# Delta-rule heads: the norm rows of a head taken two quarters at a time early in the next head, the decay sums in other banks, four K tiles ahead of the first head's sums

## What is computed

```python
def gated_deltanet(q, k, v, z, b, a, conv_w, a_log, dt_bias, norm_w):
    qkv = jax.nn.silu(causal_conv(jnp.concatenate([q, k, v], axis=-1), conv_w))
    qc = l2norm(qc.reshape(shp)) * (DN_HEAD_DIM ** -0.5)
    kc = l2norm(kc.reshape(shp))
    beta = jax.nn.sigmoid(b)
    g = -jnp.exp(a_log) * jax.nn.softplus(a + dt_bias)
    o = chunk_gated_delta_rule(qc, kc, vc, g, beta)
    o = o * lax.rsqrt(jnp.mean(o * o, axis=-1, keepdims=True) + EPS) * norm_w
    o = o * jax.nn.silu(z)
    return o

def chunk_gated_delta_rule(q, k, v, g, beta):   # per chunk
    g = jnp.cumsum(g, axis=-1)
    decay = jnp.exp(jnp.where(tril, g[..., :, None] - g[..., None, :], -jnp.inf))
    L = jnp.where(strict, (k_beta @ k.T) * decay, 0.0)
    T = triangular_solve(eye + L, eye)
    ...                                         # then the scan over the chunks
```

## Time and profile before

| | |
|---|---|
| median of 3 runs | 2531.49 us (2530.45 to 2532.93) |
| the profiled execution, its own time | 2530.18 us |
| its span | 2528.4 us |
| PE busy | 2388.7 us, 94% |
| DVE busy | 1877.6 us, 74% |
| ACT busy | 943.8 us, 37% |
| POOL busy | 1068.0 us, 42% |
| mean granted clock of TensorE | 0.985 |

### The profile page before, as it was taken

One profiled execution on the slowest core, in us unless ns is written; L12 is line 12 of the kernel. 1 busy time (PEld: TensorE's weight loads), 2 busy tenths in 40 slices (PEclk: granted clock), 3 DMA queues, 4 the chain that ended last, 5 costly groups with the idle time before them and its releaser, 6 DMA issues.

```text
span 2528.4 us, 38471 instructions
## 1 busy us (share of the span) xinstructions
PE 2388.7 (94%) x15284; PEld 1902.2 (75%) x15284; DVE 1877.6 (74%) x2356; ACT 943.8 (37%) x1488; POOL 1068.0 (42%) x675
## 2 busy tenths in 40 slices
PE   8887999899999999999999999999999999999997
PEld 6655777677788877888777778787777888778885
DVE  3675565545877889888947677777568878888887
ACT  3154223214433343443514244445243333344433
POOL 3411222234455554544544433333445555455542
PEclk9999999999999999999999999999999999999999
DMA  4200000211244465435112111111314444644332
GB/s 162 71 18 13 29 25 27 84 43 42 100 145 161 149 219 209 150 128 171 44 59 98 48 40 36 34 35 43 111 40 142 142 147 166 237 167 150 126 126 99
DMA packets 109709, 254.99 MB, mean 101 GB/s; under 512 B 9312, under 2 KB 9568, under 8 KB 107360
## 3 DMA queue, kind: packets, MB, share of 16 engines
q1 hardware_dynamic: 104112, 233.82, 27.3%
q10 hardware_dynamic: 5424, 18.75, 2.2%
HBM read 182.28 MB, written 67.63 MB: 99 GB/s over the span
## 4 chain that ended last, share of the span: by engine, by line
PE 29%; DVE 15%; issue 3%; DMA 2%; ACT 1%; SPq 1%; POOL 0%; DVEq 0%; ACTq 0%
PE pairs L680 20%; PE mid L680 8%; DVE work L1756 3%; DVE res L1756 3%; DVE tmp L1756 2%; DVE work_r L1756 2%; DMA w_raw<-w_up 2%; DVE w_raw L1756 1%; DVE tmp L2176 1%; DVE work L2143 1%; DVE x_lo L1760 0%; DVE x_lo L1756 0%; SPq L534 0%; ACT res L1269 0%; DVE res L2636 0%
## 5 line engine op out<-in xcount | busy, mean ns | idle before, releaser
L680 PE MATMUL pairs<-x_hi,w_hi 128*128 128x512 f32 x1592 | 548.1, 409 | 42.3 <-DVE x_lo L1760 15.5
L680 PE MATMUL pairs<-x_lo,w_hi 128*128 128x512 f32 x1592 | 533.0, 399 | 0.8 <-issue 0.8
L680 PE MATMUL pairs<-x_hi,w_lo 128*128 128x512 f32 x1592 | 529.0, 397 | 0.3 <-issue 0.3
L680 PEld LDWEIGHTS pairs<-x_hi,w_hi 128*128 128x128 f32 x1592 | 288.6, 191 | 124.2 <-issue 41.8
L644 POOL TENSOR_TENSOR idle<-idle 128x1 f32<-128x1 f32 x78 | 18.4, 236 | 792.9 <-PE pairs L680 783.8
L680 PEld LDWEIGHTS pairs<-x_hi,w_lo 128*128 128x128 f32 x1592 | 300.7, 191 | 64.5 <-issue 0.4
L680 PEld LDWEIGHTS pairs<-x_lo,w_hi 128*128 128x128 f32 x1592 | 300.4, 191 | 62.5
L680 PE MATMUL pairs<-work_r,w_hi 128*128 128x512 f32 x1072 | 329.9, 391 | 6.1 <-DVE work_r L1756 2.1
L663 POOL TENSOR_TENSOR w_lo<-w_raw,w_hi 128x512 fp32r<-128x512 f32 x150 | 238.0, 1596 | 230.2 <-ACT w_hi L1269 230.1
L680 PE MATMUL mid<-work_r,w_hi 128*128 128x512 f32 x992 | 310.0, 394 | 16.9 <-DVE work_r L1756 11.7
L663 POOL TENSOR_TENSOR w_lo<-work,w_hi 128x512 fp32r<-128x512 f32 x128 | 177.9, 1391 | 216.6 <-ACT w_hi L1269 216.6
(11 more groups left out here) (217 smaller groups left out, 3907.4 us busy)
## 6 DMA issues: line engine op xcount, KB each, us to landing
h_ops<-work SPq DMA_DIRECT2D x224, 256.0 KB, 4.3
w_raw<-w_stream SPq DMA_DIRECT2D x81, 512.0 KB, 3.5
w_raw<-w_up SPq DMA_DIRECT2D x120, 256.0 KB, 3.8
out_sq<-h_ops SPq DMA_DIRECT2D x28, 1024.0 KB, 5.1
x_lo_raw<-h_ops SPq DMA_DIRECT2D x28, 1024.0 KB, 5.1
work<-w_down SPq DMA_DIRECT2D x16, 1024.0 KB, 7.1
out_sq<-w_down SPq DMA_DIRECT2D x8, 1024.0 KB, 7.3
x_lo_raw<-w_down SPq DMA_DIRECT2D x8, 1024.0 KB, 5.4
```

The source lines that it names most:

```text
L680: return nc.tensor.matmul(out, w, x, start=start, stop=stop)
```

## The change

The change touches the first stage of each head.

- **Norm rows.** `dn_out_rows(h, half)` now takes two of the four quarters: two matmuls into banks 0 and 1, the first half in columns 0 to 255 and the second half in columns 256 to 511. The second half waits for the first one's end. In all of heads 1 to 3 both halves stand right after `fill(0)`, with one pass of `fill(1)` between them. `dn_normed` multiplies all four quarters at once and stands right after `dn_gated` (heads 1 and 2), or after `split_some(1, 2)` (last head). After the last head the same split is used.
- **Decay sums** go to `mid23` and no longer to `mid01`; they wait for ACT's two Ln and no longer for DVE's reading of `mid01`.
- **Order of the sums.** `dn_out_sums(h - 1)` stands ahead of the sums of q and k. ACT does `dn_out_norm(h - 1)` first, and then Ln, Ln, Exp, Exp in place of Ln, Exp, Ln, Exp.
- **Head 0** has `fill(0)` to `fill(3)` ahead of its first sums, and so fewer fills behind them.
- **Fills.** Three fills (7, 8, 9) now stand between `att` and the levels in all heads; two stand between the rows and the transposes (one in head 0).
- **Last head, DVE.** Tile 0 is split before `dn_gated`, tiles 1 and 2 behind it, then `dn_normed`, tiles 3 and 4, `dn_take`, tile 5, and tile 6 behind the two decay operations. ACT's copy of tile 6 stands ahead of its decay Exp.

```diff
@@ PE
-            def dn_out_rows(h, first):
-                pe.wait_ge(s["o_act"], bump(h, 3, 3))
-                pe.wait_ge(s["o_step"], bump(h, 2, 2))
-                quarter_rows(first, tmp[:, 0, :], s["o_sum_psum"])
+            def dn_out_rows(h, half):
+
+                if half == 0:
+                    pe.wait_ge(s["o_act"], bump(h, 3, 3))
+                    pe.wait_ge(s["o_step"], bump(h, 2, 2))
+                else:
+                    pe.wait_ge(s["o_sum_psum"], bump(h, 3, 2))
+                for b in range(2):
+                    q = 2 * half + b
+                    ins = mm(mid[:, b, half * QUARTER:(half + 1) * QUARTER], ones[32 * q:32 * q + 1, :],
+                             tmp[32 * q:32 * q + 1, 0, 0:QUARTER], True, True)
+                ins.then_inc(s["o_sum_psum"], 1)
...
+                if h:
+                    dn_out_sums(h - 1)
+                else:
+                    fill(0, 1, 2, 3)
                 pe.wait_ge(s["dn_act"], bump(h, 6, 2))
                 quarter_sums(3, CONV[0], s["ssum_psum"])
                 quarter_sums(3, CONV[1], s["ssum_psum"], QUARTER)
                 if h:
-                    dn_out_sums(h - 1)
-                fill(0)
+                    fill(0)
+                    dn_out_rows(h - 1, 0)
+                    fill(1, passes=(0,))
+                    dn_out_rows(h - 1, 1)
+                    fill(1, passes=(1, 2))
                 if last:
-                    pe.wait_ge(s["dn_act"], bump(h, 6, 5))
-                    dn_out_rows(h - 1, 0)
-                fill(1)
-                if not last:
                     fill(2)
-                if h:
-                    pe.wait_ge(s["o_step"], bump(h, 2, 1 if last else 0))
                 pe.wait_ge(s["g_set"], bump(h, 2, 1))
+                pe.wait_ge(s["dn_act"], bump(h, 6, 4))
...
-                fill(*((2,) if last else (3, 4)))
+                fill(*{0: (4,), DN_H - 1: (3,)}.get(h, (2, 3)))
...
-                fill(*range(3 if last else 5, 7))
+                fill(*range(5 if h == 0 else 4, 6))
...
-                fill(8)
-                if h and not last:
-                    pe.wait_ge(s["att"], bump(h, 1, 1))
-                    dn_out_rows(h - 1, QUARTER)
-                fill(9)
+                fill(7, 8, 9)
@@ DVE
                 else:
+                    split_some(0)
                     dn_gated(h - 1)
-                    split_some(0, 1, 2)
-                    if last:
-                        dn_normed(h - 1, 0)
+                    split_some(1, 2)
+                    dn_normed(h - 1)
+                    split_some(3, 4)
```

95 lines of the change are left out of this document (41 added, 54 removed).

## The result

| | before | changed |
|---|---|---|
| median of 5 runs | 2532.93 us (2530.45 to 2537.73) | 2521.02 us (2515.85 to 2528.83) |
| profiled execution, its own time | 2530.18 us | 2521.18 us |
| span of it, granted clock | 2528.4 us, 0.985 | 2519.4 us, 0.987 |

The ratio is 0.9945, with an interval of 0.993 to 0.996: 0.55% faster, or 10 to 18 us. The two profiled executions differ by 9.0 us. The five runs of the changed kernel spread over 13 us, those of the kernel before over 7 here and over up to 12 beside the experiments, so the last few microseconds can't be read from one profile.

What follows compares the result with a forecast made beforehand. PE is busy for 94% of the span, so the gain lies in its idle or lower-clock time in the heads' first stages. 0.5 + 3.6 + 4.6 + 7.0 = 15.7 us off 2530.18 gives 2514.5, plus 1.3 is 2515.8; range 2507 to 2524.

Steps and rivals of the forecast that it cites:

- the signs named in advance: Trace signs: no 3.2 us wait in heads 1 and 2, two `x_lo` waits, last head's first stage 42 to 46 us.
- Heads 1 and 2, the stall: Ahead of the levels: with `dn_normed` earlier, short operations finish before POOL's operation, so the 3.21 us wait goes.
- Heads 1 and 2, the clock: First levels: the lower clock goes with the stall, gaining 1.4 us in head 1 and 2.4 in head 2.
- Row groups: Norm rows: two groups of two matmuls in place of four cost 0.3 us more a head, bounds 0 and 0.7.
- POOL beside the first levels: Levels: POOL's long operation now overlaps them and holds DVE's first convolution step, costing 0.7 us, between 0 and 2.
- Head 0: Four fills moved into idle PE, less new waits, POOL beside the convolutions and in the levels: gain 0.5, bounds -2 and +3.
- Last head: First stage: waits of 1.6 (ACT's square), 3.4 (tiles 3 and 4), 2.6 (tile 6) and other costs remain; gain 7.0 us.
- Rival 2: Waits go, last head's clock stays low, POOL holds DVE fully in levels, twice in head 0's convolutions: 2524; chance 0.13.
- 17.3 us: Last head's first stage: what can be recovered, 12.3 us of idle PE plus 5.0 lost to the lower clock.
- Rival 1: All heads: POOL's collisions with DVE don't happen and the lower clock doesn't come back: 24.6 us gained, 2507; chance 0.15.
- Rival 3: Stall ahead of the levels returns; last head's gain is eaten in head 0: within 5 us of before; chance 0.05.
- rival 4: DVE's queue: `dn_normed` waits for PE's second half of rows, delaying work behind it: slower, 2537 or more; chance 0.05.

Runs made afterwards that it cites:

- e3_last_before: Changed kernel with the last head's fills, splits and ACT's copy of tile 6 in the order of before: 2529.72 us, ratio 0.9987.
- e6_h0_conv: Changed kernel with head 0's fills in the order of heads 1 and 2, its first fill waiting for the convolutions: 2516.11 us, ratio 0.9936.
- e7_splits: Changed kernel with the last head's tile 3 split ahead of `dn_normed` and tile 6 ahead of the decay operations: 2514.89 us, ratio 0.9922.
- The thick levels: Changed kernel with one fill of heads 0 to 2 moved from ahead of the levels into them, three passes at three places: 2520.42 us, ratio 0.9950.
- e5_tap0: Changed kernel with the v convolution's first step ahead of the wait for the first level's product in all heads: 2523.02 us, ratio 0.9949.
- e12_all_thick: Changed kernel with v convolution's first step early, head 0's first fill behind convolutions, tiles 3 and 6 split early, three passes at three level places: 2507.06 us.

## Why the prediction was right in the whole and wrong in its terms

The forecast was 15.7 us; the ratio says 10 to 18, the medians 11.9, the profiles 9.0. The sign, the place of the main gain and the range held. So did the signs named in advance: no wait of 3.2 us in heads 1 and 2, where the longest new one is 0.77, first levels of 4.2 us in head 1 (335.83 to 340.03), two waits for `x_lo` in the last head, a first stage of 43.96 us there, and no wait of PE between the two halves of the rows. The terms, with the lengths of the table above (the 1.57 us for ACT's square end head 2's stretch there and are counted to the last head):

| | forecast | profile | how |
|---|---|---|---|
| head 0 | +0.5 | -2.2 | 95.20 to 97.36 |
| head 1 | +3.6 | +2.1 | 83.54 to 81.40 |
| head 2 | +4.6 | +2.4 | 84.99 to 84.14 - 1.57 |
| last head | +7.0 | +5.8 | 173.23 to 165.87 + 1.57 |

1. **Heads 1 and 2, the stall: right, with a looser reason.** The 3.21 us went, by the route foretold (short operations through before POOL's). The late `dn_normed` with three fills showed that the move of `dn_normed` wasn't needed for it; the third fill did it, which I had only as a companion.
2. **Heads 1 and 2, the clock: the step that failed.** I counted 1.4 and 2.4 us of lower clock as gained with the stall. In head 1 the clock did rise, from 0.97 to 1.00 over levels and scan, and PE's busy time fell by 1.0 (54.62 to 53.60); but its idle time rose by 1.3 (1.9 to 3.2), by the wait of 0.52 beside POOL and by "issue" gaps (0.3 to 1.0), and the stretch takes 56.85 in place of 56.54. In head 2 the clock is 0.97, where it was 0.95, and nothing is gained in this profile. In those of `e3_last_before`, `e6_h0_conv` and `e7_splits`, which have the same heads 1 and 2, head 2 does run at 1.00 and PE is busy for 53.8 to 54.1 in place of 56.14, so the clock's own share is near the 2.4 forecast, and the stretch is 1.1 to 1.4 us shorter than before (less the 1.57). But their head 1 is 1.0 to 1.5 longer. Over both heads the sum had 3.8 of clock less 1.4 for POOL, a gain of 2.4 behind the first stages; in these four profiles it is between 0.3 gained and 0.3 lost. What took its place is for the most part the "issue" gaps. The wait ahead of the levels had not kept these away: in head 0, at full clock in both kernels, that wait fell from 1.50 to 0.21 and the gaps are the same (0.79 and 0.46, then 0.76 and 0.47), at the same matmuls. In head 1 before, the first levels ran at 0.66 and the first gap was missing, so there the gap came with the faster clock (0.25 us, at 344.39). The thick levels show what this was worth: 1.5 us in head 1 against this profile, 2.2 to 2.7 against the others with the same head.
3. **Row groups: 0.3 was too little.** A group of two takes 0.70 us, one of four 0.71, one of eight 1.15: the second group costs 0.6 to 0.8, about the upper bound. So two cost as much as four, and my line through four and eight was wrong. Over the four places that is 1.2 to 2.0 us more than in my sum.
4. **POOL beside the first levels, 0.7 each: right in size by luck.** DVE's TENSOR_SCALAR took 2.68 and 2.69 us beside POOL in heads 1 and 2 (0.75 alone), held to the end of POOL's 2.38; PE waited 0.52 for it. Moving it away (`e5_tap0`) took the wait and showed no gain in time. In the last head it cost nothing: its rest is 121.06 us with one row group, as before.
5. **Head 0: +0.5 was too good.** Of the new waits I had 4.0 us and the trace has 3.5 (1.26, 1.17, 0.88, 0.21), but DVE beside POOL cost 2.9 and not 1.9, since two operations were hit: 0.85 on the three steps beside `w_hi` and 2.1 on the TENSOR_SCALAR beside `w_lo`. To the levels that is -0.3. The other 1.9 lie in levels and scan, where the granted clock is 0.97 in place of 1.00: 0.03 x 58.32 / 0.5 = 3.5 us at half speed, 1.7 lost. In `e7_splits`, whose head 0 is the same, this stretch ran at 1.00 and still took 57.77 us, with 3.9 idle against 2.9 before (in `e3_last_before` 57.49, also at 1.00). So the lower clock there comes and goes with the same instructions, and without it some 1.1 to 1.4 are still lost, 0.5 to 0.75 of that to longer "issue" gaps. The prediction's bounds for head 0 went from -2 to +3.
6. **Last head: the waits right, the clock not.** Forecast 1.6, 3.4 and 2.6; measured 1.57, 2.24 and 2.27, at the tiles named, and the 2.54 ahead of the levels gone. Of DVE's two splits beside POOL, 4.11 together, only the first was held, and tile 4 was ready at 487.7 (483.55 + 4.11), 0.6 before the 488.3 foretold. The lower clock was forecast at 1.4 us (0 to 5) and cost 5.0, PE's busy time here less that in `e7_splits` (39.45 - 34.47), or 3.4 in the kernels where this stage had 0.92. That was the largest single error. Rival 2 had this half right: the clock stayed low, though POOL holding DVE in the levels cost little. Of the operations held here, the splits and the short operations have two operands in SBUF (4.11 us for two splits, 2.90 for two short ones in the earlier trace rows); the TENSOR_SCALAR has one tensor operand there, `work` or `res`, and was held as long (2.68, 2.88). The prediction's 17.3 us and its rival 2 count 5.0 us of work lost to the lower clock in this stage before. No run shows that term; what they show is PE busy for 39.92 us at 0.87 before and for 34.47 at 1.00 in `e7_splits`, with 207 matmuls each: 5.4.
7. **The whole.** The errors of the four terms sum to 7.6 us by the profiles, all of one sign; the median misses the forecast by 5, the ratio by less. One execution of each kernel can't say which is nearer: the changed kernel's own runs lie 13 us apart.

Rival 1 (2507) asked for the lower clock and DVE's collisions to go; that took the further edits of `e12_all_thick`, at 2507.06. Its ground held: the two DVE operations that read PSUM beside POOL's operation of 316.31 to 318.70 in the changed kernel, `dn_normed` (316.41) and `dn_take` (317.55), took their 1.22 us each. Rival 3 failed at the last head, rival 4 at DVE's idle time: `dn_normed` waits 4.06 us for PE in head 1 with nothing late behind it.

## What to carry to other kernels

When a stage has several waits and runs partly at the lower clock, taking out some of them may give back little more than the waits; here the clock was fully back (1.00 in place of 0.88) only when one wait of 0.9 us was left in place of 2.24 and 2.27, and it was worth as much as the waits (3.6 us of waits and 3.4 to 5.0 of clock in `e7_splits`). Before the clock behind a stall is counted as gained, look at what comes next: here PE at the full clock ran 128 matmuls of the levels in 3.3 us, where an instruction packet came about every 3.5, and the gaps (0.3 to 1.0 us in head 1) and the collision (0.52) took what the clock gave. Three passes of long matmuls among the short ones removed these gaps, 1.5 us or more in head 1 by the profile. And a fill moved into idle time also moves what it triggers on other engines: four fills gained nothing beside the convolutions, and one of them behind the convolutions shortened the stretch by 4 us.

## What was not expected of the hardware

- PE stands still for 0.2 to 1.6 us at a time in dense runs of 32x32 products, waiting for nobody that the profile shows. The gaps stand at the same instructions from kernel to kernel (in head 1 12 or 13 matmuls into a group of 64, 11 where a fill more stands ahead) and 128 or 256 matmuls apart; they go when three more passes of long matmuls stand among them.
- A group of two row-tiled matmuls of 1x256 takes 0.70 us, four 0.71, eight 1.15.
- A TENSOR_SCALAR of 128x1024 on DVE, 0.75 us alone, takes 2.7 to 2.9 us when it starts 0.2 to 0.5 us behind the start of POOL's TENSOR_TENSOR, 2.25 at 0.7 behind (254.09), and 1.2 beside POOL's TENSOR_SCALAR in `e5_tap0` (0.75 at 293.90 in the changed kernel); POOL's own operation takes 2.4 to 2.8. Three SCALAR_TENSOR_TENSOR beside POOL's TENSOR_SCALAR took 4.77 in place of 3.92.
